# Row sums of the modulation rows: 32 columns of ones in four column tiles, then a spread by 24 transfers

## What is computed

```
mod_lat = (silu(c) @ w_mod + b_mod)[:, None, :]
sh1, sc1, g1, sh2, sc2, g2 = split(mod_lat, 6)
x = x + g1 * rmsnorm(m_lat, norm_post_mix)
v = modulate(rmsnorm(x, norm_pre_ffn), sh2, sc2)      # u * (1 + sc2) + sh2
x = x + g2 * rmsnorm(moe(v), norm_post_ffn)
```

## Time and profile before

| | |
|---|---|
| median of 3 runs | 1285.39 us (1285.33 to 1285.39) |
| the profiled execution | 1285.41 us, span 1283.5 us, mean granted TensorE clock 0.991 |
| PE busy | 1229.5 us (96%) |
| PE weight loads | 558.6 us (44%) |
| DVE / ACT / POOL busy | 361.8 / 221.0 / 43.8 us |
| moved by DMA | 476.54 MB, mean 371 GB/s |

### The profile page before, as it was taken

One profiled execution on the slowest core, in us unless ns is written; L12 is line 12 of the kernel. 1 busy time (PEld: TensorE's weight loads), 2 busy tenths in 40 slices (PEclk: granted clock), 3 DMA queues, 4 the chain that ended last, 5 costly groups with the idle time before them and its releaser, 6 DMA issues.

```text
span 1283.5 us, 13946 instructions
## 1 busy us (share of the span) xinstructions
PE 1229.5 (96%) x5726; PEld 558.6 (44%) x5726; DVE 361.8 (28%) x640; ACT 221.0 (17%) x373; POOL 43.8 (3%) x90
## 2 busy tenths in 40 slices
PE   6999999999999999998999999999999989999997
PEld 3445688888443333333333333333333333333333
DVE  4567787342361112111111121112111111211113
ACT  3166631110241001010000010101110000101011
POOL 2000000240000000000000000000000000000000
PEclk9999999999999999999999999999999999999999
DMA  9732568997399999999999999999999999999995
GB/s 352 266 127 81 197 213 305 347 386 282 126 404 412 428 426 434 432 427 426 430 431 431 434 423 427 418 429 427 427 431 428 429 434 432 429 428 432 423 424 213
DMA packets 70062, 476.54 MB, mean 371 GB/s; under 512 B 6704, under 2 KB 38640, under 8 KB 47504
## 3 DMA queue, kind: packets, MB, share of 16 engines
q1 hardware_dynamic: 64032, 454.23, 85.8%
q0 software_dynamic: 3456, 21.24, 4.4%
q10 hardware_dynamic: 2512, 0.21, 0.2%
HBM read 474.60 MB, written 1.05 MB: 371 GB/s over the span
## 4 chain that ended last, share of the span: by engine, by line
PE 66%; DMA 24%; ACT 5%; DVE 4%; issue 1%; ACTq 0%; DVEq 0%; SPq 0%
PE bank L961 24%; DMA arena<-in_exp_w 24%; PE bank L976 12%; PE bank L809 11%; PE bank L1017 3%; PE bank L912 2%; PE bank L729 2%; PE bank L667 2%; PE bank L1063 1%; PE bank L922 1%; PE bank L745 1%; PE bank L695 1%; ACT arena L1171 1%; ACT arena L1165 1%; ACT arena L1173 1%
## 5 line engine op out<-in xcount | busy, mean ns | idle before, releaser
L961 PE MATMUL bank<-arena,temps 128*64 128x512 f32 x2112 | 471.3, 602 | 29.6 <-DMA arena<-in_exp_w 29.6
L961 PEld LDWEIGHTS bank<-arena,temps 128*64 128x64 f32 x2112 | 151.3, 139 | 331.1 <-issue 278.5
L976 PE MATMUL bank<-arena,vtokb 128*64 128x512 f32 x1024 | 226.8, 595 | 0.1
L1729 DVE TENSOR_SCALAR vtokb<-bank 128x512 f32<-128x512 f32 x33 | 22.8, 692 | 674.1 <-PE bank L961 674.1
L976 PEld LDWEIGHTS bank<-arena,vtokb 128*64 128x64 f32 x1024 | 70.6, 137 | 133.5 <-issue 128.0
L809 PE MATMUL bank<-arena 128*128 128x256 f32 x512 | 111.2, 379 | 0.0
L1280 ACT ACTIVATE vtokb<-vtokb 128x512 f32<-128x512 f32 x33 | 20.8, 630 | 507.1 <-DVE vtokb L1729 507.1
L809 PEld LDWEIGHTS bank<-arena 128*128 128x128 f32 x512 | 97.5, 190 | 14.8 <-issue 1.9
L1017 PE MATMUL bank<-vtokb,hot 64*128 64x512 f32 x256 | 63.6, 615 | 0.0
L745 PE MATMUL bank<-arena 128*128 128x512 f32 x128 | 56.3, 593 | 0.4 <-ACT arena L1166 0.4
L1292 ACT ACTIVATE vtokb<-bank 128x512 f32<-128x512 f32 x32 | 19.1, 597 | 204.1 <-PE bank L976 204.1
(11 more groups left out here) (283 smaller groups left out, 879.2 us busy)
## 6 DMA issues: line engine op xcount, KB each, us to landing
arena<-in_exp_w SPq DMA_DIRECT2D x115, 2048.0 KB, 22.6
arena<-in_exp_w SPq DMA_DIRECT2D x36, 4096.0 KB, 32.8
arena<-in_w_in SPq DMA_DIRECT2D x20, 1024.0 KB, 6.1
arena<-in_w_mod POOLq DMA_DIRECT2D x16, 1024.0 KB, 7.6
arena<-in_w_mod SPq DMA_DIRECT2D x16, 512.0 KB, 10.9
arena<-in_exp_w SPq DMA_DIRECT2D x8, 1024.0 KB, 22.5
arena<-in_w_pool_proj SPq DMA_DIRECT2D x4, 1024.0 KB, 13.1
arena<-in_w_rnn_proj SPq DMA_DIRECT2D x4, 1024.0 KB, 9.2
```

Source lines behind the costliest of these rows:

```text
L961: last = mm(psum[4 + q][h * SLOTS:(h + 1) * SLOTS, :], xg[:, kx // 4, kx % 4, :], w1_at[s][:, r, o:o + HALF], start=False, stop=(k == KT - 1))
L976: last = mm(psum[6][h * SLOTS:(h + 1) * SLOTS, :], actT[:, c, r, :], w2_at[s][:, r, h * HALF:(h + 1) * HALF], start=(c == 0 and r == 0), s ...
L1729: v.tensor_scalar(glu, psum[4][:, :], LIMIT, None, ALU.min).then_inc(glu_ready, 1)
```

## The change

The six `rs` jobs become two. Job 0 takes the four halves of `g1` and `sh2`: four products, each with 32 columns of the ones as weights, which write the sum of their half to 32 partitions of the bank (0 to 31, 32 to 63, and so on), each in a column tile of its own. Job 1 does the same for the two halves of `sc2` on partitions 0 to 63. ACT copies each bank once, into `rowsum[0]` (the tile `hot`) or `rowsum[1]` (a part of `RB`), waits for its own copy, and issues transfers of 32 partitions x 512 f32 (64 KB) from SBUF to SBUF: every half goes to the four groups of 32 partitions of its row. That is 16 transfers after job 0 and 8 after job 1, all on ACT's queue. DVE's wait ahead of line 1533 is no longer for ACT's copy but for all 24 transfers (`sums_landed`). SP's wait ahead of `w_out` is for `rs` 1 in place of `rs` 5.

```diff
--- before.py
+++ after.py
@@ -83,7 +83,7 @@
     for kind in ("gg", "mr", "mp"):
         plan += [(kind, c, "A") for c in range(4)]
     plan += [("pw", g, "A") for g in range(4)]
-    plan += [("rs", n, "A") for n in range(6)]
+    plan += [("rs", n, "A") for n in range(2)]
     plan += [("pp", c, "V") for c in range(4)]
     plan += [("rp", c, "V") for c in range(4)]
     for t in range(TT):
@@ -167,7 +167,8 @@
 
         acc = [slot(ACC), slot(ACC + 1)]
         row = {"g1": slot(ROWS_AT, D), "sc2": arena[:, ROWS_AT * CW + D:(ROWS_AT + 1) * CW], "sh2": b2buf[:, :], "g2": g2row[:, :]}
-        ACC_ROWS = [("g1", "sh2"), ("sc2", "g2")]
+        ACC_ROWS = [("g1", "sh2"), ("sc2",)]
+        rowsum = [hot[:, :], RB[:, 512:1024]]
 
         o = WIN * CW
         GP = 2 * ROWS * PROW
@@ -250,7 +251,7 @@
         high_ready, rest_ready, mid_ready, low_ready = (sem(n) for n in ("high_ready", "rest_ready", "mid_ready", "low_ready"))
         cnt_done, cnt_read = sem("cnt_done"), sem("cnt_read")
         ct_done, ct_read = sem("ct_done"), sem("ct_read")
-        brow_landed, rows_ready = sem("brow_landed"), sem("rows_ready")
+        brow_landed, rows_ready, sums_landed = sem("brow_landed"), sem("rows_ready"), sem("sums_landed")
         half_used, half_landed = sem("half_used"), sem("half_landed")
         tail_half = {c: sem(f"tail_half{c}") for c in (3, 5)}
         tail_third = sem("tail_third")
@@ -497,7 +498,7 @@
                     sp.wait_ge(job_done, number["pw", 3] + 1)
                     load_expert(0, 0, 1)
                 if n == chunk_no["rp", 0]:
-                    sp.wait_ge(job_done, number["rs", 5] + 1)
+                    sp.wait_ge(job_done, number["rs", 1] + 1)
                     sp.wait_ge(g2_part, 1)
                     for c in range(4):
                         sp.dma_start(wo_w[c], I["w_out"][0, c * 256:(c + 1) * 256, :].rearrange(
@@ -821,7 +822,9 @@
                     end_job(last)
                 elif kind == "rs":
                     pe.wait_ge(gm_done, 16)
-                    end_job(mm(b[:, :], ones[:, :], acc[n // 4][:, n % 4 * HALF:(n % 4 + 1) * HALF], start=True, stop=True))
+                    for q in range(2 * len(ACC_ROWS[n])):
+                        last = mm(b[32 * q:32 * q + 32, :], ones[:, 0:32], acc[n][:, q * HALF:(q + 1) * HALF], start=True, stop=True)
+                    end_job(last)
                 elif kind == "vt":
                     t, q = n // 2, n % 2
                     if n == 0:
@@ -1203,10 +1206,17 @@
                                        scale=vecT[:, c:c + 1])
                 ins.then_inc(read_act, 1)
 
-            for n in range(6):
+            for n in range(2):
                 b = job_of("rs", n)
-                r = row[ACC_ROWS[n // 4][n % 4 // 2]]
-                a.activation(r[:, n % 2 * HALF:(n % 2 + 1) * HALF], b[:, :], ACT.Copy).then_inc(read_act, 1)
+                used = 64 * len(ACC_ROWS[n])
+                a.activation(rowsum[n][0:used, :], b[0:used, :], ACT.Copy).then_inc(read_act, 1)
+                act.wait_ge(read_act, read_at[number["rs", n]][1])
+                for m, g in enumerate(ACC_ROWS[n]):
+                    for half in range(2):
+                        p = 32 * (2 * m + half)
+                        for to in range(0, P, 32):
+                            act.dma_start(row[g][to:to + 32, half * HALF:(half + 1) * HALF],
+                                          rowsum[n][p:p + 32, :]).then_inc(sums_landed, 16)
             a.activation(stat[:, 16:18], ones[:, 0:2], ACT.Sqrt).then_inc(act_warm, 1)
             act.wait_ge(act_warm, 1)
             act.wait_ge(rows_ready, 1)
@@ -1528,7 +1538,7 @@
             v.tensor_tensor(g2row[:, :], acc[1][:, D:2 * D], nrow["g2"], ALU.mult)
             link(v.tensor_tensor(brow["g2"][0:1, :], brow["g2"][0:1, :], nrow["g2"][0:1, :], ALU.mult))
             v.tensor_tensor(g2row[0:1, :], g2row[0:1, :], brow["g2"][0:1, :], ALU.add).then_inc(g2_part, 1)
-            dve.wait_ge(read_act, read_at[number["rs", 5]][1])
+            dve.wait_ge(sums_landed, 16 * 24)
             for g in ("g1", "sh2", "sc2"):
                 ins = v.tensor_tensor(row[g], row[g], brow[g], ALU.add)
             link(ins)
```

## The result

The changed kernel takes 1289.0 us (median of 13 runs, 1286.35 to 1292.21) where the kernel before takes 1285.33 beside it: ratio 1.0025, interval 1.0018 to 1.0032. The medians are 3.7 us apart (by the ratio it is 3.2 us), where 1.9 us less was forecast. The time lies outside the range (1281.9 to 1287.6) and on the other side.

A forecast was written before the change was run, and what follows sets the result against it. PE's front end was taken to set the expert weight stream's start and so the end. PE's 3.35 us gain, cut by the delayed `rp` 1 load to net -1.9 us, gave 1285.4 - 1.9 = 1283.5 us, range 1281.9 to 1287.6.

The forecast's parts named there:

- the end follows the front: PE's front end before 347.91 starts the expert weight stream; each microsecond gained or lost there moves the end equally.
- Part 1: Row sums on PE: 1.8 us in column tiles in place of 5.15, a gain of 3.35 us.
- Parts 2 and 3: ACT: six copies become two, at no cost; 24 issues of 0.64 us, last at 274.1, landing 6.3 us later.
- L: Landing time of the last of the 24 transfers: 280.4 taken, ends 270.1 and 284.4.
- my own formula: Row gate through DVE's wait ahead of `rp` 0: shift of L + 6.9 - 289.7.
- The estimate from the 0.95 us for 64 KB: Alternative for the 24 transfers: 24 x 0.95 = 22.8 us from 258.7, landing at 281.5, shift -1.3 us.
- Part 4: DVE's new wait: rows at 286.5, PE waits 0.9 us, net -2.4; ACT's later `sh2T` work keeps over 5 us cover.
- Part 5: Transfers' 1.57 MB delay `rp` 1's weight load by 4.1 us (bounds 0 to 8.2) to 294.8; last gate, net -1.9 us.
- C: Rival: rows come late enough to eat the gain, L = 284.4, `rp` 0 at 291.3, +1.6 us, 1287.0 us; chance 0.20.
- D: Rival: ACT's queue served slowly, one transfer per 1.21 us, last landing 292.8, +10.0 us, 1295.4 us; chance 0.12.

The follow-up runs named there:

- c2: Kernel before with three fill products (2.65 us of PE work) ahead of the first `rp` product; 1288.67 us, ratio 1.0023.
- e1: Changed kernel without its 24 transfers, DVE waiting for ACT's copies instead; 1283.08 us, ratio 0.9978 to the kernel before.
- e6: Changed kernel with each of the 24 transfers cut to 128 of its 512 columns; 1283.64 us, ratio 0.9985 to the kernel before.
- e3: Changed kernel with four fill products (3.5 us of PE work) in place of PE's stop ahead of `rp` 0; 1288.24 us, ratio 1.0024 to the kernel before.
- e4: Changed kernel with SP's four `w_out` pieces issued behind `w_rnn_proj` piece 1 instead of piece 0; 1287.47 us, ratio 1.0014 to the kernel before.
- e9: Changed kernel with its 24 transfers reading same-shape pieces of `w_mod` from HBM instead of SBUF; 1291.18 us, ratio 1.0039 to the kernel before.
- e7: Changed kernel with row sums in two column tiles of 64 and six transfers into 64 partitions; 1284.36 us, ratio 0.9988 to the kernel before.
- e10: Changed kernel with the same bytes in six SBUF-to-SBUF transfers over 128 partitions instead of 24 over 32; 1284.62 us, ratio 0.9991 to the kernel before.

## Why the prediction was wrong, point by point

- **What bounds the kernel, and that the end follows the front:** right (c2, e1). +3.04 us of front, +3.7 at the end.
- **Part 1, the sums:** right, 1.84 us measured for 1.8.
- **Parts 2 and 3, the issues:** 0.64 us an issue was right (median 0.61), and so was the last issue at 274. **The landing was mis-sized:** 9.5 us after its issue and not the 6.3 that I took, inside my bounds (up to 10.3). I had excused these transfers from the slow end because they are 32 long rows; in e6, with a quarter of the bytes, the last landed after 6.1 us, so the bytes of the long rows were what made them slow. With L = 283.4 my own formula gives +0.6 us, and the start of `rp` 0 came out at +0.74. The estimate from the 0.95 us for 64 KB put the last landing at 281.5. That figure of the Trainium skill ("DMA: Bandwidth & Descriptors", Bandwidth) is for loads from HBM into 128 partitions, and the page calls transfers under 64 KB dominated by descriptors, not those of 64 KB. No run has a load of that form; these 24 landed 0.80 us apart.
- **Part 4, cover of the router's row:** right; PE did not wait there (L803 follows at once).
- **Part 5, the load as a gate:** the mechanism was right, and piece 1 did become a gate. **This is the step that failed: the term was taken at half its size.** 1.57 MB cost 8.8 us of SP's queue, not 4.1. I named twice the bytes as the upper bound but held the plain price for likely, and no row of the kernel before bears on that choice. The landing moved from 290.7 to 299.2. By this alone the shift is 299.2 + 0.36 - 296.7 = +2.9 us (the changed kernel's work stood 0.36 us earlier in its span), and e3 shows that it stands alone.
- **What was left out:** a stop of PE has a second price. After 3.8 us without work the clock fell to its lower level for 3.4 us, 1.7 us of work. Every gate in my sum should have had this behind it. Here it was hidden by the load; in e4 it was not, and cost 3.0.
- **The rivals:** C had the direction, with too low a price since it knew only the rows; the sign given for it, L1533 at 284 or later, was missed by half a microsecond (283.45). D's mechanism (the queue served at one transfer per 1.21 us) did not happen: 24 landed in 283.4 - 264.9 = 18.5 us, 0.80 each.

## What to carry to other kernels

A transfer into few partitions (32 or 64 here) is not small change beside a full weight stream: cost its bytes twice and look at what stands behind them in the other queue, not only at who waits for them. Work taken off the bounding engine is only a gain if the longest path that takes its place has slack; count the stop and the clock after the stop. Where two gates lie within a microsecond or two, remove both in one experiment, or each will seem harmless.

## What the runs showed of the hardware that I had not expected

- Bytes written to 32 or 64 partitions pushed out 2.1 to 2.2 times as many bytes of the other queue; over 128 partitions 1.0 times (e9, e7, e10).
- An issue on ACT's queue took 0.61 us (median) from SBUF in the changed kernel, and 0.44 us with the source in HBM at the same shape. The eight into `b2buf` took 5.12 us there and 3.75 here:

```profile
263.59 3.75 ACTq L1218 DMA_DIRECT2D b2buf<-in_w_mod  x8
```

- SP's issues were long where its queue was behind. Four `w_out` issues took 14.4 us in the changed kernel, 5.4 in e1 and 2.8 in the kernel before; the piece issued just ahead of them landed after 19.5, 10.3 and 7.7 us. Issued later, in e4, they did not bring ACT's transfers in sooner.
- From one execution to the next the same SP queue stood some 3 us apart (17.5 to 20.7 us from issue to landing of one piece), before the change had any part in it.
- The clock fell with stops of 3.8, 5.2 and 3.0 us (changed kernel, e4, e7), and not with those of 2.3 us in e3, 2.1 us in e10 and 0.9 us in e6. In e9 it stayed up after the first stop, of 2.9 us, and fell after the second, of 4.0 us.
